# Attention scores of a one-core Trainium2 kernel: one fp32 product replaced by three fp32r products of split keys and queries

## What is computed

```python
h = rmsnorm(x, g_mix)
z = h @ w_in
u, q, k, v, gl = jnp.split(z, SPLITS, axis=-1)
a = pool_mix(u, pool_prefix, pos0, w_pool_grp, pool_scale)
...
s = jnp.einsum('bnqkgd,bnskd->bnkgqs', qb, kk).astype(jnp.float32) * ATTN_SCALE
...
p = sink_softmax(s, mask, sinks).astype(v.dtype)
o = jnp.einsum('bnkgqs,bnskd->bnqkgd', p, vv)
...
ga, gb = jnp.split(jax.nn.sigmoid(gl), N_BRANCHES, axis=-1)
mixed = ga * (a @ w_branch_pool) + gb * (o @ w_branch_attn)
x = x + mixed @ w_out
f, conv_state = conv_ffn(x, conv_prefix, g_ffn, w_up, conv_w, conv_b, w_down)
```

## Time and profile before

| | |
|---|---|
| median of 3 runs | 1375.19 us (1374.82 to 1376.34) |
| the profiled execution's own time | 1375.92 us |
| its span, first to last instruction | 1374.1 us |
| TensorE busy | 1339.8 us (98%) |
| VectorE busy | 849.1 us (62%) |
| ScalarE busy | 578.9 us (42%) |
| GpSimd busy | 112.1 us (8%) |
| mean granted TensorE clock | 0.993 |

### The profile page before, as it was taken

The page is one execution under the profiler, slowest core; times in us unless marked ns, Lnnn a source line. Parts: engine busy times, 40 slices in busy tenths (PEclk is TensorE's granted clock), DMA queues, the critical chain, the costliest instruction groups (busy, mean ns, idle before and its releaser), DMA issues.

```text
span 1374.1 us, 22665 instructions
## 1 busy us (share of the span) xinstructions
PE 1339.8 (98%) x9201; PEld 1305.7 (95%) x9201; DVE 849.1 (62%) x1070; ACT 578.9 (42%) x926; POOL 112.1 (8%) x287
## 2 busy tenths in 40 slices
PE   5999999999999999999999999999999999999996
PEld 4999989899989999999999999999999999999996
DVE  5323554544456554468888888888888865443542
ACT  5212235334542113454544545545545554344332
POOL 1000100000000001211111111110111200000000
PEclk9999999999999999999999999999999999999998
DMA  9211022121216434322132231231322489457462
GB/s 255 74 47 36 18 66 79 65 78 63 79 65 193 143 111 128 113 85 74 48 95 65 78 95 56 87 92 51 94 70 73 153 302 309 140 162 228 141 207 66
DMA packets 183507, 150.57 MB, mean 110 GB/s; under 512 B 16823, under 2 KB 169995, under 8 KB 183378
## 3 DMA queue, kind: packets, MB, share of 16 engines
q1 hardware_dynamic: 183418, 149.33, 34.8%
HBM read 118.43 MB, written 31.98 MB: 109 GB/s over the span
## 4 chain that ended last, share of the span: by engine, by line
PE 92%; DVE 4%; DMA 1%; ACT 1%; issue 1%; SPq 0%; DVEq 0%; ACTq 0%
PE PS L849 34%; PE PS L1201 32%; PE PS L1342 12%; PE PS L1295 6%; PE PS L868 2%; PE PS L992 1%; PE PS L1015 1%; PE PS L1002 1%; PE PS L1326 1%; DMA da_raw<-act_scratch 1%; DMA xtok<-in_x_prompt_dram 1%; PE PS L967 1%; PE PS L882 1%; PE PS L1144 0%; DVE a_lo L2066 0%
## 5 line engine op out<-in xcount | busy, mean ns | idle before, releaser
L1201 PE MATMUL PS<-y_lo,s_hi 128*128 128x272 f32 x528 | 152.3, 288 | 0.0
L849 PE MATMUL PS<-h_hi,up_hi 128*128 128x364 f32 (+1 forms) x576 | 132.2, 338 | 0.0
L849 PE MATMUL PS<-h_hi,up_lo 128*128 128x364 f32 (+1 forms) x576 | 127.4, 329 | 0.0
L849 PE MATMUL PS<-h_lo,up_hi 128*128 128x364 f32 (+1 forms) x576 | 127.0, 328 | 0.0
L1804 DVE TENSOR_TENSOR up_lo<-raw,up_hi 128x1024 fp32r<-128x1024 f32 x42 | 60.5, 1442 | 99.2 <-ACT up_hi L1382 99.2
L1342 PE MATMUL PS<-a_hi,wm_hi 128*128 128x384 f32 (+1 forms) x352 | 115.0, 327 | 1.8 <-DVE a_lo L2346 1.8
L1342 PE MATMUL PS<-a_hi,wm_lo 128*128 128x384 f32 (+1 forms) x352 | 113.9, 323 | 0.0
L1342 PE MATMUL PS<-a_lo,wm_hi 128*128 128x384 f32 (+1 forms) x352 | 113.8, 323 | 0.0
L849 PEld LDWEIGHTS PS<-h_hi,up_hi 128*128 128x128 f32 x576 | 97.1, 188 | 10.8 <-issue 10.0
L1201 PE MATMUL PS<-yb_hi,a_hi 128*128 128x272 f32 x352 | 101.3, 288 | 1.7 <-DVE a_lo L2066 1.1
L1201 PE MATMUL PS<-t_hi,s_hi 128*128 128x272 f32 x352 | 102.5, 291 | 0.0
(11 more groups left out here) (302 smaller groups left out, 3496.3 us busy)
## 6 DMA issues: line engine op xcount, KB each, us to landing
raw<-in_w_up_dram SPq DMA_DIRECT2D x44, 512.0 KB, 4.0
wm_raw<-in_w_down_dram SPq DMA_DIRECT2D x32, 704.0 KB, 4.7
raw<-in_w_in_dram SPq DMA_DIRECT2D x22, 512.0 KB
act_scratch<-conv_val SPq DMA_DIRECT2D x22, 512.0 KB, 4.7
dw_raw<-in_w_down_dram SPq DMA_DIRECT2D x22, 512.0 KB, 4.0
gates_scratch<-gate_st SPq DMA_DIRECT2D x16, 546.0 KB, 2.8
gates<-gates_scratch SPq DMA_DIRECT2D x16, 546.0 KB, 4.3
y_scratch<-xT SPq DMA_DIRECT2D x8, 544.0 KB, 2.7
```

Source lines behind the costliest of these rows:

```text
L849: ins = pe.matmul(PS[:, 3 * s + piece, 0:width], w[:, first_k + n, :], x[:, k, first:first + width], start=(n == 0 and q == 0), stop=(n == ...
L1201: ins = pe.matmul(PS[:, bank, 0:HALF], w[:, k, :], f(q % 2, k), start=start and k == 0 and t == 0, stop=k == KH - 1 and t == 2, skip_group ...
```

## The change

The scores are made of three products, high*high, high*low and low*high, of fp32r operands that TensorE sums in PSUM. `qblk` and `kblk` become fp32r and are written by ScalarE (`stage_high`); two new tiles, `qlow` and `klow`, lie in the place of `vT` and are written by VectorE (`stage_low`). GpSimd's `stage_qk` is gone; it keeps the copies of the values and of the new tokens' queries. ScalarE's copies for block 0 stand behind the last entry of the projection, those for block n+1 behind the exponentials of block n's second score round, that is, ahead of the sigmoid of its first gate. VectorE's for block 0 stand ahead of its first softmax, those for block n+1 at the start of block n's second half. A wait of VectorE for its own `d_done` is dropped. In the diff, lines of the kernel after are 3 to 27 higher than those before.

```diff
--- before.py
+++ after.py
@@ -255,7 +255,7 @@
         wgrp = at("wgrp", [P, NG, P])
         vnew = at("vnew", [P, DEC_B, P])
         qblk_at = at.at
-        qblk = at("qblk", [P, NQ, WIN])
+        qblk = at("qblk", [P, NQ, WIN], F32R)
         upack = at("upack", [P, NG, NSAMP])
         qpack = at("qpack", [P, DEC_B, NQ, DEC_T])
         sprob = at("sprob", [P, 2, SKEYS])
@@ -325,6 +325,9 @@
         vT_at = at.at
         vT = at("vT", [P, TP])
         gmix_b = Place(vT_at, ROW)("gmix_b", [P, D])
+        low = Place(vT_at, ROW)
+        qlow = low("qlow", [P, NQ, WIN], F32R)
+        klow = low("klow", [P, 2 * WIN], F32R)
         vtok_at = at.at
         vtok = at("vtok", [P, 1 + NBLK, P])
         cst = Place(vtok_at, 4608)("cst", [P, 6, P])
@@ -336,7 +339,7 @@
         prob = at("prob", [P, NQ, 2 * WIN])
         probT_at = at.at
         probT = at("probT", [P, 2, NQ * P])
-        kblk = at("kblk", [P, 2 * WIN])
+        kblk = at("kblk", [P, 2 * WIN], F32R)
         vblk_at = at.at
         vblk = at("vblk", [P, 2, P])
         pst = Place(prob_at, 4096)("pst", [P, POOL_W])
@@ -489,9 +492,9 @@
         dve_step = sem("dve_step")
 
         pool_step, const_done, uzero_done = sem("pool_step"), sem("const_done"), sem("uzero_done")
-        qk_staged, v_staged, sq_added, pads_done = (sem("qk_staged"), sem("v_staged"), sem("sq_added"),
+        qk_top, qk_staged, v_staged, sq_added, pads_done = (sem("qk_top"), sem("qk_staged"), sem("v_staged"), sem("sq_added"),
                                                                sem("pads_done"))
-        u_packed = sem("u_packed")
+        u_packed, q_packed = sem("u_packed"), sem("q_packed")
 
         block = ctx.enter_context(nc.Block())
 
@@ -986,11 +989,12 @@
 
                     pe.wait_ge(qk_staged, n + 1)
                     for c in range(2):
-                        for kv in range(2):
-                            v = slice(kv * HD, (kv + 1) * HD)
-                            slot = 2 * kv + c
-                            ins = pe.matmul(aux[:, slot * 2 * WIN:(slot + 1) * 2 * WIN], qblk[v, 2 * h + c, :],
-                                            kblk[v, :], start=True, stop=True)
+                        for t, (q, k) in enumerate(((qblk, kblk), (qblk, klow), (qlow, kblk))):
+                            for kv in range(2):
+                                v = slice(kv * HD, (kv + 1) * HD)
+                                slot = 2 * kv + c
+                                ins = pe.matmul(aux[:, slot * 2 * WIN:(slot + 1) * 2 * WIN], q[v, 2 * h + c, :], k[v, :],
+                                                start=(t == 0), stop=(t == 2))
                     return ins
                 return emit
 
@@ -1019,6 +1023,8 @@
 
             def sample_scores(h):
                 def emit():
+                    if h == 0:
+                        pe.wait_ge(q_packed, 1)
                     for kv in range(2):
                         v = slice(kv * HD, (kv + 1) * HD)
                         for i in range(4):
@@ -1459,6 +1465,14 @@
                                    accum_out=ssum[:, c:c + 1])
                 act.activation(sesink[:, :], sesink[:, :], ACT.Exp).then_inc(exp_done, 1)
 
+            def stage_high(n):
+
+
+                if not (isinstance(n, int) and n == 0):
+                    act.wait_ge(aux_full, aux_scores(n * 2 - 1) + 1)
+                copy(qblk[:, :, :], qT[:, :, bass.ds(n * WIN, WIN)])
+                copy(kblk[:, :], kT[:, bass.ds(n * WIN, 2 * WIN)]).then_inc(qk_top, 1)
+
             def sample_exps(h):
                 act.wait_ge(ssmax_done, h + 1)
                 for kv in range(2):
@@ -1472,6 +1486,8 @@
                         sample_exps(kv)
                     if not (last and kv):
                         exps(n * 2 + (kv + 1))
+                        if kv == 0 and not last:
+                            stage_high(n + 1)
                     else:
                         for k in range(4):
                             branch_input(k)
@@ -1488,6 +1504,9 @@
                     act.wait_ge(h_read, k + 1)
                 copy(ao_hi[:, k, :], uext[:, k, 0:TP] if k < 4 else qT[:, k - 4, :]).then_inc(ao_hi_done, 1)
 
+            act.wait_ge(proj_done, 13)
+            act.wait_ge(const_done, 2)
+            stage_high(0)
             exps(0)
             gate_block(0, True, False)
             with act.Fori(0, 6) as i:
@@ -1935,7 +1954,6 @@
                     c = FIRST_CHUNK[kind] + n + 2
                     if f < 12:
                         split_lo(c % 2, c + 1)
-            dve.wait_ge(d_done, NG)
             split_lo(1, CHUNK_GATE + 2)
 
             def score_max(rnd, scores, msk, out, sink, g, done):
@@ -1960,6 +1978,13 @@
                 link(dve.reciprocal(srec[:, 0:g], sden[:, 0:g]))
                 dve.tensor_tensor(out, out, srec[:, 0:g].unsqueeze(2).to_broadcast([P, g, out.shape[-1]]), ALU.mult)\
                     .then_inc(done, 1)
+
+            def stage_low(n):
+
+                dve.wait_ge(qk_top, n + 1)
+                dve.tensor_tensor(qlow[:, :, :], qT[:, :, bass.ds(n * WIN, WIN)], qblk[:, :, :].bitcast(F32), ALU.subtract)
+                dve.tensor_tensor(klow[:, :], kT[:, bass.ds(n * WIN, 2 * WIN)], kblk[:, :].bitcast(F32), ALU.subtract)\
+                    .then_inc(qk_staged, 1)
 
             def take_new_k():
                 take(AUX_K)
@@ -2010,6 +2035,8 @@
 
             def gate_block(n, first, last):
                 for kv in range(2):
+                    if kv and not last:
+                        stage_low(n + 1)
                     if first:
                         sample_part(kv)
                     else:
@@ -2024,6 +2051,7 @@
                         softmax(n * 2 + (kv + 1), (kv + 1) % 2, (mask_first if first and kv == 0 else mask)[:, :])
 
 
+            stage_low(0)
             dve.wait_ge(u_out, 16 * 9)
             softmax(0, 0, mask_first[:, :])
             gate_block(0, True, False)
@@ -2464,14 +2492,6 @@
                                        samples(uext[:, g, :], USAMP, PSTATE + DEC_T))
             ins.then_inc(u_packed, 1)
 
-            def stage_qk(n, rnd):
-
-                pool.wait_ge(aux_full, rnd + 1)
-
-                pool.wait_ge(uzero_done, 1)
-                pool.tensor_copy(qblk[:, :, :], qT[:, :, bass.ds(n * WIN, WIN)])
-                pool.tensor_copy(kblk[:, :], kT[:, bass.ds(n * WIN, 2 * WIN)]).then_inc(qk_staged, 1)
-
             def stage_v(n, rnd):
                 if rnd is not None:
                     pool.wait_ge(aux_full, rnd + 1)
@@ -2481,16 +2501,12 @@
 
             pool.wait_ge(proj_done, 11)
             for b in range(DEC_B):
-                pool.tensor_copy(qpack[:, b, :, :], qT[:, :, SEQ + b * DEC_T:SEQ + (b + 1) * DEC_T])
-            pool.tensor_copy(qblk[:, :, :], qT[:, :, 0:WIN])
-            pool.wait_ge(proj_done, 13)
-            pool.tensor_copy(kblk[:, :], kT[:, 0:2 * WIN]).then_inc(qk_staged, 1)
+                ins = pool.tensor_copy(qpack[:, b, :, :], qT[:, :, SEQ + b * DEC_T:SEQ + (b + 1) * DEC_T])
+            ins.then_inc(q_packed, 1)
             pool.wait_ge(aux_free, AUX_V + 1)
             stage_v(0, None)
-            stage_qk(1, aux_scores(1))
             stage_v(1, aux_values(1))
             with pool.Fori(0, 6) as i:
-                stage_qk(i + 2, aux_scores(i * 2 + 3))
                 stage_v(i + 2, aux_values(i * 2 + 3))
```

## The result

| | before | changed kernel |
|---|---|---|
| median, 6 runs each | 1375.76 us (1374.77 to 1377.97) | 1380.66 us (1378.59 to 1381.54) |
| the profiled execution's own time | 1375.92 us | 1381.54 us |
| its span | 1374.1 us | 1379.5 us |
| TensorE, ScalarE, VectorE, GpSimd busy, us | 1339.8, 578.9, 849.1, 112.1 | 1340.6, 585.3, 856.2, 101.1 |

The ratio, with its 95% interval, is 1.0031 [1.0021, 1.0042]: 0.31% slower, 2.9 to 5.8 us at 1375 (the two medians differ by 4.9). A second set, 8 runs beside 25 of the kernel before, gave 1.0026 [1.0015, 1.0037], or +3.6 us. The forecast was +3.0 us and 1378.2 us. The sign is right; the first median lies 0.7 us above the range's upper end of 1380.0, that of the second set, 1380.1, 0.1 above it.

A forecast was written before the change was run, and what follows sets the result against it. The prediction took TensorE, busy for 98% of the span, to bound the kernel. Its terms, -2.5 + 3.3 + 1.3 + 0.85 = +2.95, say +3.0 us, gave 1378.2 us against the median of 1375.19, range 1375.8 to 1380.0.

The forecast's parts named there:

- TensorE's clock after that wait: Behind the first score round's wait, TensorE runs at half clock for 3.3 or 3.4 us: +1.3 us (0.7 to 1.6).
- The score rounds, -2.5 us: TensorE's 16 score rounds: twelve fp32r matmuls in overlapping pairs take 0.91 us instead of 1.06, 0.15 less each.
- Without overlap: Rival, score rounds: fp32r pairs don't run side by side, rounds 0.56 us longer, +14.5 in all, 1389.7 us; chance 0.08.
- The first score round, +3.3 us: At the first round, TensorE waits for ScalarE's copies and VectorE's subtractions behind the last pooling group: 3.0 to 3.6 us.
- the clock holds: Rival, first gate product: no low clock behind the first wait, sum +1.65, 1376.8 us, no measurable change; chance 0.18.
- Block 0, +0.85 us: ScalarE's two copies ahead of block 0's table load make TensorE's wait for the probabilities longer by 0.6 to 1.0 us.
- The later blocks, nothing: In later blocks, waiting time already there covers ScalarE's and VectorE's added staging, so it costs TensorE nothing.
- The sum: Whole kernel: -2.5 + 3.3 + 1.3 + 0.85 = +2.95, say +3.0 us, giving 1378.2 us.
- The rival that the rounds are much faster, or that the first one doesn't wait,: Rival, score rounds: faster than their columns say, or no first wait (then -1.65 us, no change); chance 0.06.

The follow-up runs named there:

- first experiment: Changed kernel with block 0's staging moved forward (queries copied behind the value chunk, keys behind the key chunk): 1375.91 us, ratio 1.0001 to the kernel before.
- second experiment: Changed kernel with block 1's staging moved behind the chain of block 0, the first wait left as it is: 1379.25 us, ratio 1.0029 to the kernel before.
- both moves: Changed kernel with block 0's staging moved forward and block 1's behind block 0's chain: 1373.84 us, ratio 0.9985 to the kernel before; again 1374.74 us, 0.9990.

## Where the prediction was right, and which step of it failed

The direction and all the places were right; the step that failed is "TensorE's clock after that wait", which was put at +1.3 us (0.7 to 1.6) and measured 2.6 in five profiles of six, since the lower clock lasted 6.8 us and not 3.4. The median came out 2.5 us above the forecast of 1378.2. Of that, 1.6 are growth of the attention's span beyond the forecast, 1.3 of them the clock, and 0.6 are luck: the kernel before had a median of 1375.76 beside the changed kernel, and 1375.19 in the three runs that the forecast started from. The rest lies in the scatter. Without the 0.6 the first median would still have been 0.1 us above the range.

- **The score rounds, -2.5 us.** Right in the mechanism: the fp32r pairs of the two key heads do run side by side, and a round of 12 takes 0.90 us against the 0.91 forecast. The gain over the whole is a bit smaller than 16x0.15: 0.142 a round where it could be measured over 13 of them, so 2.3 us. The rounds themselves differ by 0.16; the 0.02 that is missing lies in the pieces behind them and isn't explained. Without overlap a round would have taken 1.62; that rival is out. The working holds too: once the first pair is through, the pairs of a later round start 0.11 or 0.12 us apart (start us, us, what):

```profile
223.30 0.28 PE L996 MATMUL PS<-klow,qblk 64*128 64x256 f32 x2
223.42 0.28 PE L996 MATMUL PS<-kblk,qlow 64*128 64x256 f32 x2
223.53 0.28 PE L996 MATMUL PS<-kblk,qblk 64*128 64x256 f32 x2
223.65 0.28 PE L996 MATMUL PS<-klow,qblk 64*128 64x256 f32 x2
223.76 0.28 PE L996 MATMUL PS<-kblk,qlow 64*128 64x256 f32 x2
```

- The Trainium skill's rule in "TensorE: Matmul & The Clock Gate", section "Wait — 56ns, not 53.3ns?", about 62 ns for each matmul where the array's work is shorter and the sequencer's decoder is off, would have given a saving of 2.0. It did not bind here: the four steps between the five pairs above are 0.46 us together, 58 ns for each matmul, and the round takes 0.90 us where the rule would give 0.94. That the saving was 2.3 and not 2.5 has its reason in the pieces behind the rounds.
- **The first score round, +3.3 us.** Right: a wait of 3.3, and the round starts 3.39 later. Its working, operation by operation, is what the chain shows. And it doesn't come back, except where the staging moves (first experiment).
- **TensorE's clock, +1.3 us.** This is the term that failed, in its size. The forecast took one low stretch of 3.3 or 3.4 us from the earlier trace rows, less a part that falls into the wait. Where it came it was 6.8 us long, and 5.8 us of TensorE's work fell into it, at a price of 2.6 us. Both waits in the earlier trace rows were shorter than the new one, which was said, but only as a reason for the fall to come, not for what it might last. In both of them the clock fell when the wait was over; in the new one, where it fell, TensorE still had 0.6 to 0.9 us to wait (the last section has the numbers). The sum of the other terms was good: in the profile where the clock held the span grew by 1.9 us, against the 1.65 of the rival "the clock holds". That rival is thus real in one profile of six, and wrong for the other five.
- The direction given in the section "HAM oscillation — how this bites in real kernels" of the same page of the Trainium skill, that a pause sends the clock back, held in most executions with a wait of 3.1 us or more, and not in all: three profiles with waits of 3.1, 3.3 and 3.5 us have no low stretch.
- **Block 0, +0.85 us.** Right: +0.8, as the third round's +0.64 and its gain of 0.16 say, and as the second experiment gives back. The wait is 1.0 us long and not 1.3. From the start of the second round to the product behind that wait it is 12.25 us before and 12.91 after, 0.66 more: the two copies (0.52 and 0.31) less the 0.16 of the shorter round, which the forecast of 1.3 did not take off. TensorE, too, came to it 0.1 us later.
- **The later blocks, nothing.** Right: TensorE has no wait for `klow` or `up_lo` in blocks 1 to 7.
- **The sum.** Put together from what was measured it is -2.3 + 3.4 + 2.6 + 0.8 = +4.5 us, the growth of the span. The forecast had +2.95: 1.3 of the 1.55 missing are the clock, 0.2 the rounds. Against the totals' +4.3 and +3.6 us, the intervals of both sets of runs hold the forecast's +3.0.
- **The rival that the rounds are much faster, or that the first one doesn't wait,** is out as a statement on this change. As a change to be made it is the better version: with both stagings moved the span shrinks by 1.8 us.

## What to carry to other kernels

When an operand's preparation moves from an idle engine to two busy ones, look at the first use of it: in the steady state the longer chain is hidden, and the price is paid where the consumer follows its source at once. Price such a wait as its length plus a fall of the clock that may last twice as long as after a shorter wait, and keep both ends of that term in the range, nothing and the whole (here 0 and 2.6 us). And if the totals scatter by more than the effect, compare two points inside the trace between which nothing else differs.

## What the runs showed of the hardware that was not expected

- The length of the lower clock behind a wait is not set by the wait. Behind 3.1 to 3.5 us it was nothing in three profiles (3.1, 3.3 and 3.5 us) and 6.8 us in the others, never 3.4; behind 4.5 us it was 6.8, behind 6.3 us it was 10.2. Each of these low stretches began while TensorE still waited, with 0.6 to 1.8 us of the wait left, and with 4.0 left where it lasted 10.2. In the first profile of the changed kernel, where the round starts at 170.70:

```profile
167.40:169.70 2.30, 0.00 (x0) 1.00 0.00 0
169.80:170.65 0.85, 0.00 (x0) 0.50 0.00 0
```

The stretches of 3.4 us in the earlier trace rows began about 0.1 us after their waits had ended, at 20.35 and 1286.71. The profile before, around the first of them:

```profile
20.36:20.46 0.10, 0.10 (x1) 1.00 0.20 41
20.49:20.60 0.11, 0.11 (x1) 0.50 0.40 75
```

So the length went with what was left of the wait when the clock fell, which the prediction didn't look at; no run set that on purpose. And the clock falls without a wait too: 14 of the 18 profiles kept have a low stretch near 56 us or near 635 us with no idle time of TensorE over 0.3 us right ahead of it, and in one (both moves) it is 6.8 us long. What decides between nothing and 6.8 us in two executions of one program stays open. The Trainium skill, "TensorE: Matmul & The Clock Gate", section "What's actually happening", says that the stretches over which activity is judged run freely and don't start anew with the kernel. By that the clock could do differently behind the same wait in two executions, which would fit; no run here moved it on purpose.
- The start of the last pooling group differs by 4 us between executions of one program (161.4 to 165.4 us in the changed kernel). In the profiles of the changed kernel that started it near 161.5 us the early part's low stretch of 3.4 us was at about 19 us, in those that started it at 164.6 us or later it was at about 56. Whether one causes the other wasn't tried. With a scatter like that, two kernels that differ by 0.2% can't be told apart by a few runs.
